# A chunked scan's block inversion: levels two to four by 32x32 diagonal blocks on four array tiles

## What is computed

```python
sa = einsum('bhvk,bhk->bhv', state, -kk_t)
state = state * w_t + sa[..., None] * (kk_t * a_t) + v_t[..., None] * k_t
out = einsum('bhvk,bhk->bhv', state, r_t)
```

## Time and profile before

| | |
|---|---|
| median of three runs | 2426.16 us |
| profiled execution, device time | 2422.42 us |
| its span, first to last instruction | 2420.5 us |
| TensorE busy | 2271.3 us (94%), 19396 matmuls |
| VectorE, ScalarE, GpSimd busy | 1254.5, 948.3, 829.2 us |
| granted TensorE clock, mean | 0.976 |

### The profile page before, as it was taken

How to read it: one execution, slowest core, us unless ns; L and a number is a source line. 1 busy time by engine, 2 the same in 40 slices (tenths; PEclk the granted TensorE clock), 3 DMA queues, 4 the chain that set the end, 5 groups by cost and what they waited for, 6 DMA issues and landing times.

```text
span 2420.5 us, 45998 instructions
## 1 busy us (share of the span) xinstructions
PE 2271.3 (94%) x19396; PEld 1695.2 (70%) x19396; DVE 1254.5 (52%) x2027; ACT 948.3 (39%) x1665; POOL 829.2 (34%) x456
## 2 busy tenths in 40 slices
PE   8999999999978998888888898999998999999998
PEld 6886778888866647777777747877887766763476
DVE  5128254022164476777777515595313899736123
ACT  4238434233244434454445434465322222344133
POOL 2310334344413124444444203344441433330246
PEclk9999999999979998999999999999997999999999
DMA  4312222232312210000000112244221333222222
GB/s 143 118 51 77 70 70 87 104 96 82 101 36 67 96 41 10 7 8 10 8 9 10 38 61 71 94 182 139 96 87 61 131 113 113 87 87 79 70 89 85
DMA packets 49883, 180.69 MB, mean 75 GB/s; under 512 B 5601, under 2 KB 5857, under 8 KB 49441
## 3 DMA queue, kind: packets, MB, share of 16 engines
q1 hardware_dynamic: 46064, 166.89, 21.0%
q10 hardware_dynamic: 3632, 11.08, 1.1%
HBM read 167.39 MB, written 10.55 MB: 74 GB/s over the span
## 4 chain that ended last, share of the span: by engine, by line
PE 72%; issue 12%; DVE 6%; ACT 6%; POOL 3%; DMA 1%; POOLq 0%; ACTq 0%; SPq 0%; DVEq 0%
PE ps L596 15%; PE ps L597 15%; PE ps L598 14%; PE ps L599 6%; POOL ring_lo L2202 3%; PE ps L895 3%; PE ps L858 2%; PE ps L644 2%; PE ps L886 1%; PE ps L806 1%; PE ps L1072 1%; PE ps L715 1%; ACT arena L1453 1%; PE ps L1008 1%; PE ps L730 1%
## 5 line engine op out<-in xcount | busy, mean ns | idle before, releaser
L2202 POOL TENSOR_TENSOR ring_lo<-ring,ring_hi 128x1024 fp32r<-128x1024 f32 x232 | 565.2, 2444 | 1017.7 <-ACT ring_hi L1129 1017.6
L598 PE MATMUL ps<-u_lo,ring_hi 128*128 128x512 f32 x968 | 384.8, 398 | 0.0
L1129 ACT ACTIVATE ring_hi<-ring 128x1024 fp32r<-128x1024 f32 x232 | 243.1, 1053 | 108.4 <-DMA ring<-in_wall 105.0
L599 PE MATMUL ps<-arena,ring 128*128 128x512 f32 x608 | 266.1, 594 | 6.3 <-ACT arena L1573 3.3
L599 PEld LDWEIGHTS ps<-arena,ring 128*128 128x128 f32 x608 | 114.4, 190 | 154.2 <-issue 138.5
L596 PE MATMUL ps<-mlp_u_hi,ring_hi 128*128 128x512 f32 x512 | 204.9, 400 | 13.0 <-DVE u_lo L1690 8.5
L598 PEld LDWEIGHTS ps<-u_lo,ring_hi 128*128 128x128 f32 x968 | 183.8, 190 | 43.4
L596 PE MATMUL ps<-mid_hi,ring_hi 128*128 128x512 f32 x512 | 203.4, 397 | 2.6 <-POOL ring_lo L2202 2.6
L597 PE MATMUL ps<-mlp_u_hi,ring_lo 128*128 128x512 f32 x512 | 203.7, 398 | 0.0
L598 PE MATMUL ps<-mid_lo,ring_hi 128*128 128x512 f32 x512 | 202.6, 396 | 0.0
L597 PE MATMUL ps<-mid_hi,ring_lo 128*128 128x512 f32 x512 | 202.6, 396 | 0.0
(11 more groups left out here) (423 smaller groups left out, 4296.5 us busy)
## 6 DMA issues: line engine op xcount, KB each, us to landing
ring<-in_wall SPq DMA_DIRECT2D x273, 512.0 KB, 3.6
s_tables<-arena ACTq DMA_DIRECT2D x16, 512.0 KB, 2.9
arena<-s_tables SPq DMA_DIRECT2D x16, 512.0 KB, 3.6
arena<-bias_lines SPq DMA_DIRECT2D x16, 448.0 KB, 4.2
arena<-in_lora SPq DMA_DIRECT2D x8, 384.0 KB, 2.9
h<-in_x SPq DMA_DIRECT2D x1, 2048.0 KB, 8.1
out<-arena ACTq DMA_DIRECT2D x8, 256.0 KB, 2.9
consts<-in_consts SPq DMA_DIRECT2D x1, 1216.0 KB, 14.2
```

The costliest lines, as they stand in the source:

```text
L598: return nc.tensor.matmul(y, w_hi, low, start=False, stop=x == k - 1)
L599: return nc.tensor.matmul(y, ring[:, at:at + P], rhs(x), start=x == 0, stop=x == k - 1)
L1129: nc.scalar.activation(ring_hi[:, slot], ring[:, slot], ACT.Copy).then_inc(sem("weights_high"), 1)
L2202: G.tensor_tensor(ring_lo[:, slot], ring[:, slot], ring_hi[:, slot].bitcast(F32), ALU.subtract).then_inc(sem("weights_split"), 1)
```

## The change

A function `each_quarter` is new. For each of 8 chunks it makes four products of 32x32 by 32x32 (by 32x16 where `h` is given), one on each of the four 32x32 tiles along the array's diagonal: the two diagonal quarters of each head's 64x64 block. At levels 2, 3 and 4, X and dt are made by it: 32 products per call in place of 16. At level 1 dt is made by `each` over all 64 columns, which also leaves zeros in the quarters of PSUM off the diagonal that VectorE still reads; level 5 stays as it was.

```diff
+            def each_quarter(out, a, b, l, h=None):
+
+                for c in range(NCH):
+                    for e in range(4):
+                        rows, at = slice(e * 32, (e + 1) * 32), slice(c * CH + e % 2 * 32, c * CH + (e % 2 + 1) * 32)
+                        to, by = out[rows, at], b[rows, at]
+                        if h is not None:
+                            to, by = columns_of_level(to, l, h), columns_of_level(by, l, h)
+                        mm = nc.tensor.matmul(to, a[rows, at], by, start=True, stop=True)
+                return mm
...
-                        each(A[d], R[d]["LM"], R[d]["T"]).then_inc(sem("x_ready"), 1)
+                        if l in (2, 3, 4):
+                            mm = each_quarter(A[d], R[d]["LM"], R[d]["T"], l)
+                        else:
+                            mm = each(A[d], R[d]["LM"], R[d]["T"])
+                        mm.then_inc(sem("x_ready"), 1)
...
-                        each_half(B[d], R[d]["TT"], R[d]["X"], l, 1 - d).then_inc(sem("dt_ready"), 1)
+                        if l == 1:
+                            mm = each(B[d], R[d]["TT"], R[d]["X"])
+                        elif l < 5:
+                            mm = each_quarter(B[d], R[d]["TT"], R[d]["X"], l, 1 - d)
+                        else:
+                            mm = each_half(B[d], R[d]["TT"], R[d]["X"], l, 1 - d)
+                        mm.then_inc(sem("dt_ready"), 1)
```

## The result

The changed kernel takes 2495.28 us (median of four runs, 2491.13 to 2496.46) where the kernel before takes 2423.57 us (median of four runs, the three of the table above and one more): ratio 1.0292, 95% interval 1.0278 to 1.0305. It is 72 us slower.

What follows compares the result with a forecast made beforehand. Instruction fetches were taken to bound levels 2 to 4: 10.3 us more a pair less 1.9 gives 8.4, or 67 over eight pairs; 2426.2 + 67 = 2493 us, range 2466 to 2530.

Steps and rivals of the forecast that it cites:

- "issue" gaps in mid-call: TensorE stops inside calls at levels 4 and 5, 0.42 to 0.84 us, with no semaphore waited for.
- instruction blocks: Instructions are fetched in blocks of about 127 loads, 127 products and a few waits, taking 3.75 us each on average.
- The promise of the change: At levels 2 to 4, a small-tile call of 64 records would take 0.5 to 1.0 us instead of 0.92.
- The credit of half a block: At the start of level 2, part is already fetched: between nothing and 3.75 us back, taken as 1.9 a pair.
- 8.1 blocks: Levels 2 to 4 of a pair would hold 1028 records, or 8.1 blocks, asking for 30.4 us where 20.1 were measured.
- The gaps: In levels 2 to 4 of the changed kernel, mid-call "issue" gaps of 2 to 3 us would break up the small-tile calls.
- Level 5 and the rest: Level 5 would move as a whole, neither winning nor losing; masks, updates and the next pair's features would move along.
- One: Levels 2 to 4: tiles pay, up to 13 us faster (3%); weaker form, deeper prefetch keeps time within 0.3% (3%).
- Two: Levels 2 to 4: four small tiles do not overlap, staying at 29 ns a record; 72 us more, 2498 us; chance 10%.
- Three: Each pair meets half clock once or twice more, adding 15 to 30 us to the 67: 2508 to 2523 us; 15%.

Runs made afterwards that it cites:

- e1: Changed kernel with the 32x32 products of levels 2 to 4 made for four of eight chunks only; 2420.72 us, ratio 0.9993 to the kernel before.
- e3: Changed kernel with each 32x32 product moving fewer columns (X 8 of 32; dt 8, 4 or 2 of 16); 2490.87 us, ratio 1.0282 to the kernel before.
- e4: Kernel before, but at levels 2 to 4 one 64x64 load serves 128 moved columns, halving loads and products (inverse wrong); 2411.37 us, ratio 0.9954.
- e9: Changed kernel with every 32x32 product moving all 64 columns of its chunk; 2490.94 us, ratio 1.0279 to the kernel before.
- e7: Changed kernel with 32x32 products at level 4 alone; 2456.30 us, ratio 1.0143 to the kernel before.
- e2: Kernel before with every 64x64 product of levels 2 to 4 issued twice in a row; 2500.83 us, ratio 1.0322.
- e8: Kernel before with X made on TensorE and copied by ScalarE only in the columns dt reads; 2435.37 us, ratio 1.0057.
- e10: Kernel before with ScalarE copying only the columns of X that dt reads, TensorE making all of X; 2421.24 us, ratio 0.9989.

## Why the prediction was right

**Bound.** The step that decided was to read the "issue" gaps in mid-call as waits for instruction blocks. It held: three packets more in each pair, resumptions at 127 or 128 records, and e1, e3 and e4 move instructions and array work apart, the time following the instructions each time. The four packets shown above start in step with the resumptions. That a packet travels while TensorE works is seen in the kernel before too. The view of the earlier trace rows has 40 slices of 0.195 us (GB/s in each):

```profile
GB/s 84 0 0 0 0 0 0 0 0 0 0 0 0 0 0 0 0 0 0 0 84 0 0 0 0 0 0 0 0 0 0 0 0 0 0 0 0 0 0 84
```

The middle packet starts at 995.8, 1.1 us behind the resumption at 994.66, and takes about 0.030 x 16 x 7.8 / 3 = 1.25 us, while TensorE runs without a stop from 994.66 to 997.65.

**Pace of small tiles.** Put at 8 ns from the 64x64 tiles' 29 and 15 ns and the shorter load; it is 8.1 to 9.5 ns at full clock. The promise of the change was real and worth nothing.

That it is the load that occupies a tile was my estimate, and no run shows it by itself. What the runs show is the pace against the moved columns, all at full clock. On four 32x32 tiles a record of X takes 9.4 ns with 8 columns (e3, 128 records in 1.39 us, one lasting 0.19), 9.5 with 32, and 14.0 with 64 (e9, 128 records from 988.42 in 1.99 us, one lasting 0.22). On two 64x64 tiles it takes 29 ns with 64 columns and 55 with 128 (e4). So the moved columns did not set the pace up to 32 on the small tiles and up to 64 on the large ones; twice as many took 1.5 and 1.9 times as long. From two tiles of 64x64 to four of 32x32 a record became 3.1 to 3.6 times as fast, and the gaps of up to 1.88 us above took all of it.

**Size.** Levels 2 to 4 were to grow by 8.4 us a pair; in the second pair they grew by 29.4 - 20.1 = 9.3, the stage by 8.75 a pair. The block was put at 3.75 us; the three steps shown above are 3.94 to 4.09. The prediction had steps of 3.6 to 3.9, and the three are above that. The credit of half a block (1.9 us) at the start of level 2 can only be had as a remainder, and a rough one. From 989.71 to 1013.04 are six steps, 3.89 us each; 8.1 blocks at that pace would be 31.5 us, and 29.4 were measured, which leaves 2.1. In all the growth was put at 67 us and is 71.7. That 2493 lies only 2 us from 2495.28 is in part luck: it started from a median of 2426.2 us for the kernel before, which a fourth run brought down to 2423.57.

**The gaps** were put at 2 to 3 us and are 0.69 to 1.88 in the second pair. The prediction had a block worked off in about 1 us. It left out that `each_stacked` lies among the small calls and that the clock falls: the 127 records from 1001.05 take until 1004.17, 3.1 us, in the changed kernel, and 2.3 us at full clock in e9 (1003.62 to 1005.93).

**Level 5 and the rest** moved as a whole: the row at 1018.85 waits for ScalarE as the row at 1003.70 did, 3.56 us after the level's first product where it was 3.55, with part of level 5 at half clock. All else of the second pair grew by 10.0 - 9.3 = 0.7 us (the pair from 61.2 to 71.2).

**The rivals.** One (the tiles pay, or a deeper prefetch covers the blocks) falls by the result in both its forms. Two (tiles do not overlap) would have given nearly the same time, and falls by the pace. Three came half true: the clock fell in every pair, more than I had allowed for, but the price I had put on it, 15 to 30 us, was wrong in kind. Nor did longer idling go with a lower clock: e9 idles for 5.89 us in the four gaps against 4.41, at a stage clock of 0.97 against 0.81. I had taken the price from a pair in which TensorE's array was the bound; in these levels the fetch is, and e9 shows no price.

**What stays open.** The single levels cost 16.4, 27.5 and 34.3 us, more than I had worked out from the fetch count; level 4's is 4.3 us a pair, more than one block of 3.75. One thought is that large products at half clock follow the small ones. The trace of e7 does not bear it out for level 5: in the second pair its X does take 3.62 us at half clock, but dt starts 3.56 us after X's first product, where it was 3.55. The growth is in level 4 itself, 12.41 us from its first product to the first of level 5 where there were 7.41, with resumptions 3.98 and 3.97 us apart. Why a block takes 3.40 us in one place (e3) and 4.13 in another (e2) no run separates. Nor did any run show an instruction fetch with more than one block ahead, or whether the period can be shortened.

## What to carry to other kernels

Count instructions before cutting a product into smaller ones. Here each f32 product stood as four instructions (6144 more for 1536 products), and where TensorE stopped by "issue" it went on once every 127 or 128 records, 3.40 us (e3) to 4.13 us (e2) apart in the stretches shown. That is 27 to 33 ns for each load and product, measured on two tiles of the array (e2) as on four (e3, changed kernel), though the small ones run at 8.1 to 9.5 ns in between. Gaps by "issue" in the middle of a call, at a constant count of records, were the sign; what helped was fewer, larger products (e4, ratio 0.9954), not faster ones (e1, 0.9993 against the kernel before; e3, 2490.87 us beside the changed kernel's 2495.28).

## What the runs showed of the hardware that was not expected

- The two-tile pace of 29 ns a record and the block's 3.7 us for 127 of them coincide, so the kernel before sat near both limits at once. Easing the array alone won nothing (e1, 0.9993); taking instructions away at nearly the same array time won 12 us (e4).
- Moving fewer columns cost time in one run. e8 differs from e10 only in that TensorE makes half the columns of X, with as many instructions; the clock of the stage is 0.91 where e10 has 0.99, and the time is above that of the kernel before by 13 us where e10's is below it by 2. e9 moves up to four times the columns of the changed kernel and goes from 0.81 to 0.97 at no cost. Fewer columns don't always do this: e3 moves the fewest, and its stage has a clock of 0.80 and the changed kernel's time. Columns that nobody needs were cheaper than their absence in this case, by a ratio of 0.9989 (e10) against 1.0057 (e8).
- Where TensorE waits for instructions, their packets come some 4 us apart but take only about 1.35 us each, and each starts about a microsecond after TensorE has gone on. So most of a step is not transfer.
- Four 32x32 tiles take 13 ns a record at half clock, from the row at 1009.08: (0.52 - 0.20) / 24. Beside the stalls of 1.88 and 0.87 us at 1009.08 and 1013.04 even this did not show.
